# A transformer trunk's later norms: the sample part's inverse root moves from VectorE's reciprocal to a power on GpSimd

## The reference, cut to what matters

```python
def rmsnorm(x, g):
    xf = x.astype(jnp.float32)
    y = xf * lax.rsqrt(jnp.mean(xf * xf, axis=-1, keepdims=True) + EPS)
    return (y * g.astype(jnp.float32)).astype(x.dtype)
...
    h = rmsnorm(x, g_mix) * (1.0 + sc1) + sh1
    u = h @ w_in
...
    x = x + gt1 * (mixed @ w_out)
    h2 = rmsnorm(x, g_ffn) * (1.0 + sc2) + sh2
    x = x + gt2 * (jnp.square(jax.nn.relu(h2 @ w_up)) @ w_down)
```

## Time and profile before

| what | value |
|---|---|
| time, median of 3 runs | 1798.0 us (1797.81 to 1798.96) |
| profiled execution: its time | 1798.7 us |
| profiled execution: its span | 1797.1 us |
| TensorE busy | 1782.7 us, 99% |
| VectorE, ScalarE, GpSimd busy | 984.9, 734.6, 349.5 us |
| mean granted TensorE clock | 0.999 |

### The profile page before, as it was taken

The page is one execution under the profiler, slowest core; times in us unless marked ns, Lnnn a source line. Parts: engine busy times, 40 slices in busy tenths (PEclk is TensorE's granted clock), DMA queues, the critical chain, the costliest instruction groups (busy, mean ns, idle before and its releaser), DMA issues.

```text
span 1797.1 us, 35346 instructions
## 1 busy us (share of the span) xinstructions
PE 1782.7 (99%) x11933; PEld 1624.6 (90%) x11933; DVE 984.9 (55%) x1606; ACT 734.6 (41%) x1411; POOL 349.5 (19%) x459
## 2 busy tenths in 40 slices
PE   8999999999999999999999999999999999999998
PEld 7888888889999999999988888888899999999998
DVE  5466666667333575543364666666674346655333
ACT  3444444446322354522235444444463234554222
POOL 3333333330000210000023334333300003000000
PEclk9999999999999999999999999999999999999999
DMA  9878888996666734456638788888875635344432
GB/s 342 233 195 223 225 235 237 226 238 198 215 209 205 263 98 128 128 176 203 218 107 234 203 220 226 231 236 226 230 225 165 211 118 199 118 128 126 131 124 100
DMA packets 505241, 348.47 MB, mean 194 GB/s; under 512 B 201931, under 2 KB 468109, under 8 KB 505110
## 3 DMA queue, kind: packets, MB, share of 16 engines
q1 hardware_dynamic: 484992, 292.13, 56.8%
q0 software_dynamic: 12592, 44.99, 7.7%
q10 hardware_dynamic: 7526, 9.58, 1.5%
HBM read 313.56 MB, written 34.37 MB: 194 GB/s over the span
## 4 chain that ended last, share of the span: by engine, by line
PE 97%; DVE 1%; ACT 1%; issue 1%; ACTq 0%; POOL 0%; DVEq 0%
PE G L1618 50%; PE G L1654 32%; PE X L1779 8%; PE X L1677 2%; PE X L1578 2%; PE G L1894 2%; PE X L1654 1%; DVE wlo L1111 0%; DVE hp L1182 0%; DVE rstd L1172 0%; ACT hp L802 0%; PE X L1671 0%; ACTq L777 0%; POOL small L705 0%; ACT xtok L783 0%
## 5 line engine op out<-in xcount | busy, mean ns | idle before, releaser
L1111 DVE TENSOR_TENSOR wlo<-raw,whi 128x1024 fp32r<-128x1024 f32 x369 | 470.8, 1276 | 550.1 <-ACT whi L783 548.2
L783 ACT ACTIVATE whi<-raw 128x1024 fp32r<-128x1024 f32 x369 | 390.8, 1059 | 760.0 <-PE G L1618 439.2
L1654 PE MATMUL G<-whi,hhi 128*128 128x512 f32 x832 | 334.3, 402 | 1.3 <-DVE hlo L1187 0.9
L1654 PE MATMUL G<-whi,hlo 128*128 128x512 f32 x832 | 325.1, 391 | 0.0
L1654 PE MATMUL G<-wlo,hhi 128*128 128x512 f32 x832 | 324.5, 390 | 0.1
L1618 PE MATMUL G<-hhi,whi 128*128 128x384 f32 x704 | 236.9, 336 | 0.1
L1618 PE MATMUL G<-hhi,wlo 128*128 128x384 f32 x704 | 235.4, 334 | 0.0
L1618 PE MATMUL G<-hlo,whi 128*128 128x384 f32 x704 | 235.3, 334 | 0.0
L1654 PEld LDWEIGHTS G<-whi,hhi 128*128 128x128 f32 x832 | 156.1, 188 | 49.8 <-issue 13.1
L1618 PE MATMUL G<-ysp,whi 128*128 128x384 f32 x768 | 196.9, 337 | 0.0
L1654 PEld LDWEIGHTS G<-wlo,hhi 128*128 128x128 f32 x832 | 156.1, 188 | 34.1 <-DVE wlo L1111 0.6
(11 more groups left out here) (237 smaller groups left out, 2532.8 us busy)
## 6 DMA issues: line engine op xcount, KB each, us to landing
raw<-in_w_in_dram SPq DMA_DIRECT2D x256, 128.0 KB
raw<-in_w_in_dram SPq DMA_DIRECT2D x128, 256.0 KB
raw<-in_w_up_dram SPq DMA_DIRECT2D x64, 512.0 KB
raw<-in_w_down_dram SPq DMA_DIRECT2D x64, 512.0 KB
raw<-in_w_in_dram SPq DMA_DIRECT2D x49, 512.0 KB
ada_w<-in_w_ada_dram SPq DMA_DIRECT2D x44, 512.0 KB, 5.9
kc<-in_cache_attn_k_dram SPq DMA_DIRECT2D x64, 256.0 KB, 6.4
vc<-in_cache_attn_v_dram SPq DMA_DIRECT2D x32, 512.0 KB, 7.9
```

The source lines that it names most:

```text
L783: return a.activation(out, in_, ACT.Copy)
L1111: v.tensor_tensor(wlo[:, j % SPLIT, :, :], raw[:, j % RAW, :, :], whi[:, j % SPLIT, :, :].bitcast(F32), ALU.subtract).then_inc(blk_split, 1)
L1654: ins = t.matmul(B[banks[m][0]][:, :], x[:, kp * WK + k, m * P:(m + 1) * P], w[:, k, :], start=first and k == 0 and x is hhi and w is w_hi ...
```

## The change

A column of -1.0, `mone`, is put into a spare column of `mhalf` at the start. In the three later norms GpSimd itself forms the sample's `rstd` from `std`, as `std` to the power -1 over 128x128 elements, behind its scale products and ahead of its wait for itself. VectorE's reciprocal of the sample's columns goes, and the one of the prompt's raises `rstd_ready` by 2.

```diff
@@ -207,6 +207,7 @@
     mhalf = sb("mhalf", [P, 8])
+    mone = mhalf[:, NT + 1:NT + 2]
@@ -584,9 +585,11 @@
         pool.wait_ge(pool_own, 9)
+        g.memset(mone, -1.0).then_inc(pool_own, 1)
+        pool.wait_ge(pool_own, 10)
         g.affine_select(out=ident[:, :], in_=ident[:, :], compare_op=ALU.not_equal, fill=1.0, base=0,
                         pattern=[[-1, P]], channel_multiplier=1).then_inc(consts, 1)
-        pool.reg_add(cnt.regs["own"], cnt.regs["own"], 9)
+        pool.reg_add(cnt.regs["own"], cnt.regs["own"], 10)
@@ -649,8 +652,9 @@
+            pool.wait_ge(std_ready, c.norm + 1)
+            c.op(g.tensor_tensor(rstd[:, PR:TOK], std[:, PR:TOK], mone[:, 0:1].to_broadcast([P, P]), ALU.pow))
             c.settle()
-            pool.wait_ge(rstd_ready, c.norm * 2 + 1)
             for k in range(KT + 1):
                 if k < KT:
                     c.op(g.tensor_tensor(hs[:, k, :], hs[:, k, :], rstd[:, PR:TOK], ALU.mult))
@@ -1168,8 +1172,7 @@
         def inverse_std(c):
             dve.wait_ge(std_ready, c.norm + 1)
-            v.reciprocal(rstd[:, PR:TOK], std[:, PR:TOK]).then_inc(rstd_ready, 1)
-            v.reciprocal(rstd[:, 0:PR], std[:, 0:PR]).then_inc(rstd_ready, 1)
+            v.reciprocal(rstd[:, 0:PR], std[:, 0:PR]).then_inc(rstd_ready, 2)
```

## The result

Before 1798.48 us, after 1861.19 us (six runs each), ratio 1.0342 with the interval 1.0332 to 1.0352. By the medians it is 62.7 us slower; the interval of the ratio stands for 59.7 to 63.3 us. The forecast was 1891 us with 1797 to 1903. The direction, the place and the mechanism came out as said; the power lasts 20.75 us, where 31.8 had been taken.

A forecast was written before the change was run, and what follows sets the result against it. TensorE, busy 1782.7 of 1797.1 us, was taken as the bound. Three powers' delay, 3 x 31.76 - 6.63 = 88.7, + 5.1 clock - 0.7 hidden waits = 93.1 us, gave 1891 us, range 1797 to 1903.

The forecast's parts named there:

- TensorE is the bound, and a loss comes through in full: Whole kernel: TensorE busy 1782.7 of 1797.1 us; any delay beyond the filler costs everything, three times over.
- The cover of 2.22, 2.13 and 2.28 us: Three later norms: power time that costs nothing before TensorE's first product is later than now; 6.63 us in all.
- The length of the power: GpSimd, each later norm: T, 128 columns of power priced per column, 0.098 + 128 x 0.247 = 31.8 us.
- The bound with a whole multiply as the fixed part: GpSimd's power, per-column case: fixed part 385 ns, so T = 19.8 us, loss 57.2 us, time 1855.
- the dearest case: GpSimd's power priced per column with no fixed part: T = 35.8 us, loss 105.3 us, time 1903.
- the likeliest case: GpSimd's power priced per column: chance 0.50, wholly slower, own range 1850 to 1903 us.
- the mark of 20: GpSimd's power: the forecast was to be wrong if it lasted under 20 us.
- A fixed price: GpSimd's power: rival with 742 ns per instruction, T = 1.1 us, gain 0.5 to 1.2 us, 1796.8 to 1797.5; chance 0.25.
- By groups: GpSimd's power: rival priced by column groups; with 16 per group T = 6.0 us, 1810 to 1815; chance 0.24.
- Absorbed: Three later norms: rival that other engines run ahead while TensorE stands; excluded by engine order, worth under 1 us.
- The clock: TensorE's granted clock falls after each norm's wait: 1.71 us each, 5.1 charged, bounds 0 and twice; minus 0.7 for hidden waits.
- The saved reciprocal: VectorE, three later norms: `hp` of tile 0 comes 0.87 us earlier, behind filler worth at most 1.24 us.

The follow-up runs named there:

- e8_twice: The changed kernel with its power computed twice, one behind the other, each waited for: 1922.16 us against 1799.3 before, ratio 1.0694.
- e1c_price: The kernel before, plus powers and multiplies of several widths on idle GpSimd after layer 0's second norm: 1799.04 us against 1799.69, ratio 0.9998.
- e6_eight: The changed kernel with only 8 sample columns by GpSimd's power, 120 by VectorE's reciprocal ahead of the prompt's: 1799.12 us against 1799.3 before, ratio 0.9998.
- e3c_multiply: The changed kernel with a multiply by -1 in place of the power, computing other values: 1797.33 us against 1799.69 before, ratio 0.9987.
- e2c_half: The changed kernel with 64 sample columns by GpSimd's power, the other 64 by VectorE's reciprocal first: 1832.08 us against 1799.69 before, ratio 1.018.
- e7_order: Against the kernel before, VectorE inverts the prompt's columns first and the sample's second, no power, GpSimd waiting for the second: 1800.9 us against 1799.3, ratio 1.0013.

## Why the prediction was right, and where its size was off

- *TensorE is the bound, and a loss comes through in full.* This was the mechanism, and it is shown: widths 8, 64, 128 and 2 x 128 gave 0, 32, 63 and 123 us over before. With the in-place times the working "3T minus the cover" gives 31.6 - 6.6 = 25.0 and 62.2 - 6.6 = 55.6 us ahead of the clock for 64 and 128; the trace has 56.0 for 128 (and e8_twice adds the second power in full).
- *The cover of 2.22, 2.13 and 2.28 us.* Right to 0.15 us per norm: 8 columns at 1.66 us cost nothing, and the first product came 2.59 us after the power's end (653.07 to 655.66) where 2.44 had been added up; VectorE's prompt `hlo` lasted 0.62 us instead of 0.48.
- *The length of the power.* This is the step that was mis-sized: "742 / 3 = 247 ns, and T = 31.8 us". The 98 ns of a memset was taken as the price of any instruction. The fixed part of a power is 340 ns by the widths 64 and 128, which leaves 500 ns for three columns in the earlier trace rows and 159.5 ns for each over wide operations. From 3 columns an error of 242 ns in the fixed part is multiplied by 128 / 3 - 1 = 41.7, and that is 10.1 of the 11.0 us by which T was too long. Three times 11.0 is 33 us. Against it the chain cost 0.4 us more than charged and all else that makes up the 62.7 us 2.3 more (6.7 where 4.4 had been charged), so the loss of 93.1 us was forecast 30.3 us too high. The bound with a whole multiply as the fixed part (385 ns, 19.8 us) was nearly it, and came from a row nearer in kind.
- *How much the hit is worth.* The range of 1797 to 1903 reaches from no change to the dearest case, so that the time lies in it says little. The range of the likeliest case, 1850 to 1903, holds 1861 because of that lower bound, and the power of 20.75 us only just passes the mark of 20 under which the forecast was to be called wrong. The price by column was shown; that its size stayed inside the marks was partly luck.
- *A fixed price, the rival that was not slower:* out, by e1c_price, though it had a chance of 0.25. *By groups:* out above 8 columns. *Absorbed:* out, by e8_twice.
- *The clock.* It fell as said, and its price was set too low: 1.71 us per norm were taken from the start of the kernel, and the profile after has 2.6, 3.1 and 3.0 us of shortfall, 8.7 where 5.1 had been charged. Half pace hides more waits than the 0.7 us taken off, so the sum came out nearer than its terms: the traces with and without filler differ by 5.5 us (the times by 4.9), where 5.1 - 0.7 = 4.4 had been charged. The bound of twice the clock's charge was named and not carried into the upper end, which would be 1908 with it.
- *The saved reciprocal is worth nothing.* `hp` of tile 0 started 1.91 us after the inversion instead of 2.70, so 0.79 us nearer where 0.87 had been said, and stood behind the sample's copy. With a cheap stand-in for the power the kernel is 2.4 us faster (0.7 to 3.8), against "at most 1.24": compatible, not tight.

The row says 20.75 us for 128 columns of a power and 0.40 for a multiply of the same size. The Trainium skill, GPSIMD Engine Reference, section 3.1, has about 2.6 cycles at 1.2 GHz per element for `tensor_tensor`; it measured an add, and calls the figure the floor that two inputs set. By an estimate from that figure 128 columns are 0.28 us and a fixed part, and the multiply agrees; the power is 159.5 ns or, by an estimate with the page's clock, some 190 cycles per column. The measurement decides: the page's rate fits the multiply and can't be carried over to the power.

No version here that computes the reference is shown to beat the kernel before; e6_eight equals it.

## What to carry to other kernels

A small operation's duration says little of a large one's: with one size in the trace, bound the fixed part by the nearest operation of the same kind (here a two-input multiply, not a memset) and look at what the rest, multiplied up, does to the path. Before work is moved off a busy engine, ask whether that engine's time was on the path at all, and how much filler covers the new place; a cover of 2 us carries 8 columns of this power and not 128. Where a wait of TensorE can't be avoided, filling it with products can be worth the clock that it keeps.

## What the runs showed of the hardware

- GpSimd's power: 340 ns and 159.5 ns per column in float32, about the same for 16 and 128 partitions (32 columns: 5.4 and 5.7 us, single readings); its multiply of 128 columns 0.40 us.
- TensorE's granted clock was 1.00 up to 640 us and 0.50 from 641 us in layer 0's second norm, with TensorE idle since 637.01. It was back at 1.00 in the 662nd us. Its shortfall after the three stops (2.6, 3.1 and 3.0 us) stands for 5.2, 6.2 and 6.0 us of products at 0.50; at the start of the kernel it was 3.4 us. After the twice as long stops of e8_twice it was 4.1, 5.2 and 5.3 us, after the short ones of e2c_half 6.1, 3.2 and 3.8: it varies, and not with the length of the stop. What it goes by wasn't tried.
- VectorE's reciprocal of 256 columns took 1.75 us beside the power and 1.70 before. That is not the power's doing: beside the 0.40 us multiply of e3c_multiply it took the same, as its timeline shows, and 1.70 where another reciprocal stood ahead of it (e6_eight). In e7_order, without any power, it was first and took 1.75, and the one of 128 columns behind it 0.89, where it takes 0.95 when it is first. The first one behind the wait is 0.05 to 0.06 us longer.

```profile
630.04 1.75 DVE L1175 RECIPROCAL rstd<-std 128x256 f32<-128x256 f32 x1 [0.71 <-ACT std L831]
```
